# Latent attention: value products in three passes of split operands, the mask as rows, maxima and sums by transfers

## The chip, the cores and the metric

The kernel runs on one core of a Trainium2 chip. The metric is the device time of one execution in microseconds. TensorE does matrix products, VectorE (DVE), ScalarE (ACT) and GpSimd (POOL) elementwise work, and SyncE (SP) issues the transfers between the core's memory and the chip's main memory. Each engine works through its own list of instructions in order and waits on semaphores for the others.

## The reference

One layer of a streaming encoder in float32: 2048 prompt tokens and 64 sample tokens. An input projection feeds two mixers. Mixer A is latent attention (8 heads, 64 + 32 columns for scores, 64 for values), mixer B a sliding window attention. Both go through an output projection, a norm and a gated feed-forward network. The change is in mixer A:

```python
def mla_attend(qn, qp, k_nope, kpe, v, mask):
    s = (jnp.einsum('bqhd,bkhd->bhqk', qn, k_nope)
         + jnp.einsum('bqhr,bkr->bhqk', qp, kpe)).astype(jnp.float32) * MLA_SCALE
    if mask is not None:
        s = jnp.where(mask, s, NEG_INF)
    p = jax.nn.softmax(s, axis=-1).astype(v.dtype)
    return jnp.einsum('bhqk,bkhd->bqhd', p, v)
```

The mask lets a query see the keys of its own chunk of 64 tokens and of all earlier chunks. The sample tokens see 128 cached tokens and each other, without a mask.

## The kernel before

The program has three blocks, with a barrier of all engines between them: `project_inputs` (to 372 us), `attention` (to 1067 us) and `mix_and_ffn` (the rest). In `attention` the window attention comes first, then the latent attention (`latent_attention`), from 514.9 us on.

**fp32r and fp32.** A float32 product is done either as one product of kind fp32, or as three passes of kind fp32r: each operand is split into a high part, which is what fp32r keeps of it, and a low part, the rest, and high x high, high x low and low x high are added up. Projections and scores use three passes of fp32r. The value product (L1446) uses one product of kind fp32, which the trace shows as two records.

**Tiling of a head.** Queries are taken in units of 512 columns (u = 0 to 3) and one of 64 columns (u = 4, the sample), in the order 0, 4, 1, 2, 3; `pos` is the place in this order. A unit needs all key tiles of 128 up to its own last one: 42 tiles in a head, numbered s = 0 to 41. Unit 3, for instance, has tiles 26 to 41. On the diagonal a tile has 512, 384, 256 or 128 columns. So 28 tiles have 512 columns, four each have 384, 256 and 128, two have 64.

**A step.** In step s TensorE writes the scores of tile s in three passes (`score_tile`, L1426), keys on the partitions, queries along the columns; then zero to two maximum products (`max_chunk`, L1403), which are scores of a later unit with queries on the partitions and up to 512 keys along the columns, in one pass; and then the value product of tile s - 3 (LAG = 3). ScalarE takes the exponential of tile s from PSUM (L1495). There are three banks for scores, two for maximum products, two for outputs.

**Maxima.** VectorE reduces each maximum product (L1542, and L1544 for the half of a diagonal block that fewer queries see), joins the parts (L1552), TensorE turns the result into a row by four transposes (L1412) and ScalarE copies it with its sign changed into row 96 of the queries (L1486). Row 96 of the keys is one, so the score product subtracts the maximum by itself. `SPANS` says over which steps the maximum products of a unit are spread, `ROWS` at which step its row is made.

**Mask.** On a diagonal tile, GpSimd overwrites a block of 64x64 probabilities with zeros (L1387), and the value product waits for it.

**Sums.** The weights of the value product are 128 columns, the values in 64 and ones in the other 64, so its output has the head's result on 64 partitions and the sum of the probabilities on each of the other 64. ScalarE copies it out of PSUM (L1502), VectorE takes the reciprocals of 64 partitions in pieces of 128 columns (L1562), multiplies (L1571), and SyncE stores (L1347).

**Loads.** Queries, keys and values of the next head are loaded at its predecessor's step 1 with 7 transfers (`load_head`, L2274 to L2286). Heads are done in pairs: the first and last pair are written out, the two in between are a loop. At the end of the stage, ScalarE and VectorE already prepare the first tiles for `mix_and_ffn`.

## Time and profile before

| | us |
|---|---|
| median of three runs | 2862.89 |
| lowest and highest | 2862.08 to 2865.33 |
| the profiled execution | 2869.5 |
| its span | 2867.7 |
| TensorE busy in the span | 2729.4 |
| VectorE, ScalarE, GpSimd busy | 1889.1, 1306.4, 321.1 |
| latent attention, first score product to last value product's copy | 514.90 to 1060.3 |

A profile is one execution. PE is TensorE's products, PEld its weight loads, which overlap them. Records of products overlap, since each includes the way through the array: the rate is read from the distance of starts. The granted clock is TensorE's share of full speed (1.0 is 2.4 GHz). `97*128 97x512` is a product of 97 rows with 128 columns of weights and 512 moving columns. In brackets stands the idle time before an instruction and who ended it.

### The profile page before, as it was taken

What the parts mean: (1) busy time and instruction counts of PE and PEld (TensorE: products, weight loads), DVE (VectorE), ACT (ScalarE), POOL (GpSimd) and SP (SyncE); (2) the same over time, 40 slices, a digit from 0 to 9 for tenths busy, and PEclk for the clock granted to TensorE, in tenths of its full rate; (3) what the DMA queues carried; (4) which work ended last, traced back from release to release, by engine and by line L of the source; (5) the groups of instructions that cost most, each with busy time, mean ns of one, the idle gap of its engine ahead of it and who ended that gap; (6) DMA issues with size and microseconds to landing.
All of it is one profiled execution on the core that took longest, in us unless ns stands there. A gap on an engine that the chain in (4) does not pass through costs nothing.

```text
span 2867.7 us, 42705 instructions
## 1 busy us (share of the span) xinstructions
PE 2729.4 (95%) x13401; PEld 2417.4 (84%) x13401; DVE 1889.1 (66%) x2677; ACT 1306.4 (46%) x2725; POOL 321.1 (11%) x352
## 2 busy tenths in 40 slices
PE   8999978999999988999999999999999999999996
PEld 7888944666666658899999999999999999999996
DVE  6877677666666655777558754587546875468743
ACT  4443267433333434554445443454434544346531
POOL 0111021000000004000101012010120101200002
PEclk9999989899999999999999999999999999999998
DMA  7666555322223213334323533335333353324332
GB/s 220 203 204 227 188 169 154 74 55 57 55 54 62 62 63 125 103 111 143 118 96 114 183 111 116 97 111 185 113 111 104 110 182 118 112 101 136 120 122 76
DMA packets 170703, 348.65 MB, mean 122 GB/s; under 512 B 43892, under 2 KB 112852, under 8 KB 169268
## 3 DMA queue, kind: packets, MB, share of 16 engines
q1 hardware_dynamic: 170580, 347.06, 38.9%
q8 instruction: 71, 1.16, 0.2%
q14 instruction: 52, 0.43, 0.0%
HBM read 292.56 MB, written 55.30 MB: 121 GB/s over the span
## 4 chain that ended last, share of the span: by engine, by line
PE 54%; DVE 3%; issue 2%; DMA 1%; ACT 1%; POOL 1%; SPq 0%; POOLq 0%; ACTq 0%; DVEq 0%
PE mf_acc L2003 54%; DMA room<-in_w_up 1%; DVE mix_w_lo L2156 1%; ACT mix_w_hi L2049 1%; POOL mf_ss L1961 1%; PE mf_st L2041 0%; DVE mf_x L2174 0%; DMA room<-in_w_out 0%; DVE mf_xn L2207 0%; DVE mf_x L2179 0%; POOL mf_y L1986 0%; DVE mix_a_lo L2212 0%; ACT mf_sq L2072 0%; ACT mf_sq L2106 0%; DVE mf_rstd L2191 0%
## 5 line engine op out<-in xcount | busy, mean ns | idle before, releaser
L2156 DVE TENSOR_TENSOR mix_w_lo<-room,mix_w_hi 128x1024 fp32r<-128x1024 f32 (+1 forms) x338 | 470.9, 1393 | 557.8 <-ACT mix_w_hi L2049 557.1
L2003 PE MATMUL mf_acc<-mix_a_hi,mix_w_hi 128*128 128x424 f32 (+1 forms) x2016 | 724.3, 359 | 28.6 <-DVE mix_a_lo L2186 8.8
L2003 PE MATMUL mf_acc<-mix_a_hi,mix_w_lo 128*128 128x424 f32 (+1 forms) x2016 | 717.5, 356 | 0.0
L2003 PE MATMUL mf_acc<-mix_a_lo,mix_w_hi 128*128 128x424 f32 (+1 forms) x2016 | 717.1, 356 | 0.0
L2049 ACT ACTIVATE mix_w_hi<-room 128x1024 fp32r<-128x1024 f32 (+1 forms) x338 | 383.1, 1133 | 520.2 <-PE mf_acc L2003 488.9
L2003 PEld LDWEIGHTS mf_acc<-mix_a_hi,mix_w_hi 128*128 128x128 f32 x2016 | 381.8, 189 | 44.2 <-issue 11.8
L2003 PEld LDWEIGHTS mf_acc<-mix_a_hi,mix_w_lo 128*128 128x128 f32 x2016 | 382.4, 190 | 11.1
L2003 PEld LDWEIGHTS mf_acc<-mix_a_lo,mix_w_hi 128*128 128x128 f32 x2016 | 382.1, 190 | 9.3 <-issue 0.7
L1426 PE MATMUL at_ps<-ahead_q,ahead_k 97*128 97x512 f32 (+5 forms) x1008 | 362.1, 468 | 0.9 <-ACT ahead_q L1486 0.9
L2003 PE MATMUL mf_acc<-mf_h_hi,mix_w_hi 128*128 128x424 f32 (+1 forms) x944 | 339.0, 359 | 6.8 <-DVE mix_w_lo L2156 3.8
L2003 PE MATMUL mf_acc<-mf_h_hi,mix_w_lo 128*128 128x424 f32 (+1 forms) x944 | 335.2, 355 | 0.0
L2003 PE MATMUL mf_acc<-mf_h_lo,mix_w_hi 128*128 128x424 f32 (+1 forms) x944 | 334.7, 355 | 0.0
L1495 ACT ACTIVATE la_prob<-at_ps 128x512 f32<-128x512 f32 (+1 forms) x336 | 174.1, 518 | 322.0 <-PE at_ps L1426 321.4
L1446 PE MATMUL at_ps<-la_prob,ahead_v 128*128 128x512 f32 (+5 forms) x672 | 294.5, 520 | 0.0
L1426 PEld LDWEIGHTS at_ps<-ahead_q,ahead_k 97*128 97x128 f32 (+1 forms) x1008 | 180.4, 190 | 130.9 <-issue 95.7
L1542 DVE TENSOR_REDUCE la_part<-at_ps 128x1 f32<-128x512 f32 (+5 forms) x328 | 183.9, 573 | 155.7 <-PE at_ps L1403 152.9
L1961 POOL TENSOR_TENSOR mf_ss<-mf_sq,mf_ss 128x424 f32<-128x424 f32 (+1 forms) x105 | 145.5, 1386 | 478.6 <-ACT mf_sq L2072 348.7
L2003 PEld LDWEIGHTS mf_acc<-mf_h_hi,mix_w_hi 128*128 128x128 f32 x944 | 177.9, 188 | 14.8 <-DVE mix_w_lo L2156 4.9
L2003 PEld LDWEIGHTS mf_acc<-mf_h_lo,mix_w_hi 128*128 128x128 f32 x944 | 177.8, 188 | 6.1 <-issue 1.7
L2003 PEld LDWEIGHTS mf_acc<-mf_h_hi,mix_w_lo 128*128 128x128 f32 x944 | 177.7, 188 | 4.4
L768 PE MATMUL pi_acc<-pi_x_hi,pi_w_hi 128*128 128x424 f32 (+1 forms) x400 | 147.0, 367 | 22.5 <-DVE pi_x_lo L547 16.9
L2230 DVE SCALAR_TENSOR_TENSOR mf_cv<-mf_u,mf_conv_w,mf_cv 128x424 f32<-128x424 f32 (+1 forms) x220 | 145.0, 659 | 31.2 <-DVE mf_cv L2227 27.5
(186 smaller groups left out, 3542.8 us busy)
## 6 DMA issues: line engine op xcount, KB each, us to landing
room<-in_w_up SPq DMA_DIRECT2D x220, 512.0 KB, 3.5
room<-in_w_down SPq DMA_DIRECT2D x80, 704.0 KB, 4.0
pi_w_raw<-in_w_in SPq DMA_DIRECT2D x49, 512.0 KB, 6.0
room<-in_w_out SPq DMA_DIRECT2D x40, 512.0 KB, 3.5
ahead_k<-kn_scr SPq DMA_DIRECT2D x7, 1120.0 KB, 14.6
ahead_q<-qn_scr SPq DMA_DIRECT2D x7, 1056.0 KB, 7.9
room<-in_x SPq DMA_DIRECT2D x4, 1696.0 KB, 11.9
qn_scr<-pi_ring SPq DMA_DIRECT2D x16, 424.0 KB
```

The costliest lines, as they stand in the source:

```text
L768: mm = pe.matmul(acc[:, g, 0:n], w[:, s, k], x[:, par, k, 0:n], start=(k == 0 and m == 0), stop=(k == KD - 1 and m == 2))
L1426: mm = pe.matmul(out, k[0:KR, p, a, c0:c0 + keys], q[0:KR, p, b, n0 + off:n0 + n], start=(term == 0), stop=(term == 2))
L1446: pe.matmul(ov[:, (5 * p + pos) % 2, off:n], v[0:keys, p, vt], prob[0:keys, (NKT * p + s) % RING, off:n], start=(m == 0), stop=(s == last_ ...
L1495: act.activation(prob[0:keys, (NKT * p + s) % RING, off:n], sc[0:keys, s % 3, off:n], ACT.Exp, scale=MLA_SCALE).then_inc(exp_done, 1)
L1542: op = dve.tensor_reduce(part[0:rows, par, t, slot:slot + 1], sx[0:rows, bank, 0:seen], AX_X, ALU.max)
L1961: pool.tensor_tensor(ss[:, kind, 0:n], sq[:, slot, 0:n], zeros[:, 0:n] if first else ss[:, kind, 0:n], ALU.add).then_inc(sq_added, 1)
L2003: mm = pe.matmul(acc[:, t_bank[0], 0:n], w[:, g, k], x[:, k, 0:n], start=(first and k == 0 and m == 0), stop=(last and k == count - 1 and ...
L2049: act.activation(w_hi[:, g, 0:count], w_raw[:, g, 0:count], ACT.Copy).then_inc(w_hi_made, 1)
L2156: dve.tensor_tensor(w_lo[:, g, 0:count], w_raw[:, g, 0:count], w_hi[:, g, 0:count].bitcast(F32), ALU.subtract).then_inc(w_split, 1)
L2230: dve.scalar_tensor_tensor(out=out, in0=u[:, g, 1:n + 1], scalar=conv_w[:, 1, bass.ds(f, 1)], in1=out, op0=ALU.mult, op1=ALU.add).then_inc ...
```

## The change

The value product becomes three passes of fp32r with 96 columns of weights: 64 of the values' high part with 32 ones (columns 0 to 95), then 64 of the low part with 32 zeros, and the first ones again with the probabilities' low part. ScalarE takes each exponential twice, once to fp32 (`prob`, 4 buffers of which 3 are used) and once to fp32r (`high`), and one engine writes the difference (`low`): GpSimd at every third step, VectorE at the others. The values are split by ScalarE and GpSimd ahead of each head.

The mask is 16 rows more in queries and keys: row r is one in the first half of query tile r, and -2^100 in the second half of key tile r. The maximum goes to a 17th row, of which the keys hold -1. `SPANS` and `ROWS` are earlier.

The maxima are turned by VectorE in blocks of 32x32, and SyncE writes the row with four transfers (two for the sample). A unit's sum is one row, taken to the main memory (`sums_out`), back on 32 partitions (`sums_in`), inverted there, taken out again (`rec_out`) and spread over 128 partitions (`rec_in`); GpSimd multiplies, SyncE stores. These happen 1, 3, 5, 7, 9 and 10 steps after the unit's last value product. The loads of a head become 20 transfers of 8 rows, one a step, and 10 for values. In the feed-forward and in the window attention some semaphores are merged, and the last stores of the window attention move into the first steps of the latent one.

The diff, cut to this core (`prob[...]`, `high`, `low` are rings of tiles; "..." marks what is left out):

```diff
+HIDE = -2.0 ** 100
...
+V_LO = slice(V_DIM + 32, 2 * V_DIM + 32)
...
+            pool.memset(ahead["v"][:, g, :, V_DIM:V_LO.start].bitcast(F32), 1.0).then_inc(rows_set, 1)
+            pool.memset(ahead["v"][:, g, :, V_LO.stop:].bitcast(F32), 0.0).then_inc(rows_set, 1)
...
+        diagonal = ident[HD:MR, HD:MR].rearrange("r (t o) -> r t o", o=1).broadcast_to([MR - HD, SEQ // P, CHUNK])
+        for g in range(2):
+            halves = [x[HD:MR, g, 0, 0:SEQ].rearrange("r (t e c) -> r t e c", e=2, c=CHUNK)
+                      for x in (ahead["q"], ahead["k"])]
+            pool.tensor_scalar(halves[0][:, :, 0], diagonal, 1.0, None, ALU.mult).then_inc(rows_set, 1)
+            pool.tensor_scalar(halves[1][:, :, 1], diagonal, HIDE, None, ALU.mult).then_inc(rows_set, 1)
+        pool.wait_ge(rows_set, 17)
...
-    SPANS = {3: (0, 10), 4: (12, 22), 0: (24, 27), 1: (28, 28), 2: (29, 37)}
-    ROWS = {3: 12, 4: 24, 0: 31, 1: 32, 2: 39}
+    SPANS = {3: (0, 9), 4: (10, 21), 0: (22, 26), 1: (27, 27), 2: (28, 36)}
+    ROWS = {3: 10, 4: 22, 0: 27, 1: 28, 2: 37}
...
+    FIRST_OF_POOL = 9
+
+    def on_pool(i, p, s):
+
...
+    def split_low(eng, i, p, s, done):
+
+        pos, m = tiles[s]
+        _, keys, _, off = key_tiles(ORDER[pos])[m]
+        if on_pool(i, p, s):
+            keys = P
+        n, x = cols(ORDER[pos])[1], NKT * p + s
+        eng.wait_ge(exp_done, tile_no(i, p, s) + 1)
+        ge(eng, pv_done, tile_no(i, p, s) + 1 - RING)
+        eng.tensor_tensor(low[0:keys, x % RING, off:n], prob[0:keys, x % RAWS, off:n],
+                          high[0:keys, x % RING, off:n].bitcast(F32), ALU.subtract).then_inc(done, 1)
...
+        def sums_out(i, p, pos):
+            a, _, n, y = chain(i, p, pos)
+            sp.wait_ge(kept, y + 1)
+            sp.dma_start(d["sum_scr"][a:a + 1, 0:n], raw[V_DIM:V_DIM + 1, a, 0:n]).then_inc(moved[a], 16)
+
+        def sums_in(i, p, pos):
+            a, base, n, _ = chain(i, p, pos)
+            sp.wait_ge(moved[a], base + 16)
+            sp.dma_start(sums[0:n // CE, a],
+                         d["sum_scr"][a][0:n].rearrange("(c e) -> c e", e=CE)).then_inc(moved[a], 16)
+
+        def rec_out(i, p, pos):
+            a, _, n, y = chain(i, p, pos)
+            sp.wait_ge(rec_done, y + 1)
+            sp.dma_start(d["inv_scr"][a][0:n].rearrange("(c e) -> c e", e=CE), rec[0:n // CE, a]).then_inc(moved[a], 16)
+
+        def rec_in(i, p, pos):
+            a, base, n, _ = chain(i, p, pos)
+            sp.wait_ge(moved[a], base + 48)
+            row = bass.AP(tensor=d["inv_scr"].tensor, offset=a * UQ, ap=[[0, P], [1, n]])
+            sp.dma_start(rec_all[:, a, 0:n], row).then_inc(moved[a], 16)
+
         def store(i, p, pos):
...
+            sp.wait_ge(turned, 2 * y + 2)
+            ge(sp, row_in[a], 16 * (rows_of_parity(i, p, pos) - row_parts(pos)))
+            for e in range(row_parts(pos)):
+                if u < 4:
+                    to = q[MR:MR + 1, p, 0, n0:n0 + UQ].bitcast(F32).rearrange("o (t c) -> o t c", t=QT)[:, :, Q4 * e:Q4 * e + Q4]
+                    sp.dma_start(to, turned_top[Q4 * e:Q4 * e + QT, a]).then_inc(row_in[a], 16)
...
-            if s == 1 and more:
-                j, g = following(i, p)
-                ge(sp, pv_done, tile_no(i, p, 0))
-                load_head(sp, d, ahead, j, g, head_in[g], range(HEAD_DMAS))
+            for unit in rows_at(i, p, s, more):
+                row(*unit)
+            for unit in after(i, p, s, 1):
+                sums_out(*unit)
+            for unit in after(i, p, s, 3):
+                sums_in(*unit)
+            for unit in after(i, p, s, 5):
+                rec_out(*unit)
+            for unit in after(i, p, s, 7):
+                rec_in(*unit)
+            for unit in after(i, p, s, 10):
+                store(*unit)
+            if more:
+                load(i, p, s)
...
-        def max_row(i, p, pos):
-
-            y = unit_no(i, p, pos)
-            pe.wait_ge(top_done, y + 1)
-            ge(pe, row_set, y)
-            for t in range(QT if ORDER[pos] < 4 else 1):
-                mm = pe.transpose(mt[0:1, t * P:(t + 1) * P], top[:, (5 * p + pos) % 2, t:t + 1], ident[:])
-            mm.then_inc(mt_done, 1)
+            pe.matmul(sx[0:rows, (NCH * p + first_chunk[pos] + m) % 2, 0:n], q[0:MR, p, 0, q0:q0 + rows],
...
-            for term, (a, b) in enumerate(((0, 0), (0, 1), (1, 0))):
-                mm = pe.matmul(out, k[0:KR, p, a, c0:c0 + keys], q[0:KR, p, b, n0 + off:n0 + n],
+            for term, (a, b, rows) in enumerate(((0, 0, MR + 1), (0, 1, HD), (1, 0, HD))):
+                mm = pe.matmul(out, k[0:rows, p, a, c0:c0 + keys], q[0:rows, p, b, n0 + off:n0 + n],
                                start=(term == 0), stop=(term == 2))
...
-            if diag:
-                pe.wait_ge(masked, 2 * len(diagonal) * i + len(diagonal) * p + diagonal.index(s) + 1)
-            else:
-                pe.wait_ge(exp_done, tile_no(i, p, s) + 1)
-            pe.matmul(ov[:, (5 * p + pos) % 2, off:n], v[0:keys, p, vt], prob[0:keys, (NKT * p + s) % RING, off:n],
-                      start=(m == 0), stop=(s == last_tile[pos]), skip_group_check=True).then_inc(pv_done, 1)
+                ge(pe, kept, unit_no(i, p, pos) - 1)
+            if s == 0:
+                if at_first(i, p):
+                    pe.wait_ge(wa["ov_kept"], wa["tiles"])
+                    pe.wait_ge(wa["rec_kept"], wa["tiles"])
+                pe.wait_ge(v_split, 3 * (2 * i + p) + 3)
+            out, hi, lo = ov[0:V_LO.start, parity(p, pos), off:n], high[0:keys, slot, off:n], low[0:keys, slot, off:n]
+            pe.wait_ge(exp_done, tile_no(i, p, s) + 1)
+            pe.matmul(out, v[0:keys, p, vt, 0:V_LO.start], hi, start=(m == 0), stop=False, skip_group_check=True)
+            pe.matmul(out, v[0:keys, p, vt, V_LO.start:], hi, start=False, stop=False, skip_group_check=True)
+            wait_low(pe, i, p, s)
+            pe.matmul(out, v[0:keys, p, vt, 0:V_LO.start], lo, start=False, stop=(s == last_tile[pos]),
+                      skip_group_check=True).then_inc(pv_done, 1)
...
+            earlier = back(i, p, s, RAWS)
+            if earlier:
+                wait_low(act, *earlier)
+            ge(act, pv_done, tile_no(i, p, s) + 1 - RING)
+            act.activation(prob[0:keys, x % RAWS, off:n], sc[0:keys, s % 3, off:n], ACT.Exp, scale=MLA_SCALE)
+            act.activation(high[0:keys, x % RING, off:n], sc[0:keys, s % 3, off:n], ACT.Exp,
                            scale=MLA_SCALE).then_inc(exp_done, 1)
 
...
+            dve.wait_ge(turned, 2 * y + 1)
+            ge(dve, row_in[a], 16 * (rows_of_parity(i, p, pos) - row_parts(pos)))
+            dve.transpose(turned_top[:, a], top[:, a]).then_inc(turned, 1)
+
+        def invert(i, p, pos):
+            n, a = cols(ORDER[pos])[1], place(p, pos)
+            dve.wait_ge(moved[a], 80 * earlier_there(i, p, pos) + 32)
+            dve.reciprocal(rec[0:n // CE, a], sums[0:n // CE, a]).then_inc(rec_done, 1)
...
-            for i_, p_, pos, t, n in norms(i, p, s):
-                invert(i_, p_, pos, t, n)
-                if t == n - 1:
-                    norm(i_, p_, pos)
+            if at_first(i, p) and s == 6:
+                dve.memset(raw[V_LO.start:P, 0:3], 0.0)
+            if not on_pool(i, p, s):
+                split_low(dve, i, p, s, low_dve)
+            for unit in after(i, p, s, 5):
+                invert(*unit)
...
+            pool.wait_ge(moved[a], 80 * earlier_there(i, p, pos) + 64)
+            pool.tensor_tensor(raw[:, a, 0:n], raw[:, a, 0:n], rec_all[:, a, 0:n],
+                               ALU.mult).then_inc(normed, 1)
+
         def step(i, p, s, more):
-            if s in diagonal:
-                x = tile_no(i, p, s)
-                _, _, _, off, _ = key_tiles(ORDER[tiles[s][0]])[tiles[s][1]]
-                pool.wait_ge(exp_done, x + 1)
```

TensorE, first head, two steps around the start of the unit u = 1 (tile 6), before. L1426 are scores, L1403 maximum products, L1412 transposes, L1446 values:

```order
L1403 MATMUL at_ps<-ahead_k,ahead_q 128x512 [waits la_sx_free]
L1412 MATMUL at_ps<-early_ident,la_top 1x128 [waits la_row_set,la_top_done]
L1412 MATMUL at_ps<-early_ident,la_top 1x128 x3
L1446 MATMUL at_ps<-la_prob,ahead_v 128x256 [waits la_masked]
L1426 MATMUL at_ps<-ahead_q,ahead_k 128x512 [waits la_exp_done,la_row_set]
L1426 MATMUL at_ps<-ahead_q,ahead_k 128x512 x2
L1403 MATMUL at_ps<-ahead_k,ahead_q 128x128 [waits la_sx_free]
L1403 MATMUL at_ps<-ahead_k,ahead_q 128x512 [waits la_sx_free]
L1446 MATMUL at_ps<-la_prob,ahead_v 128x128 [waits la_masked]
```

The same place now, L1636 scores, L1622 maximum products, L1655, L1656 and L1658 the three passes for the values:

```order
L1636 MATMUL at_ps<-ahead_q,ahead_k 128x512 [waits la_exp_done,la_row_in0]
L1636 MATMUL at_ps<-ahead_q,ahead_k 128x512 x2
L1622 MATMUL at_ps<-ahead_k,ahead_q 128x512 [waits la_sx_free]
L1655 MATMUL at_ps<-la_high,ahead_v 96x128 [waits la_exp_done]
L1656 MATMUL at_ps<-la_high,ahead_v 96x128
L1658 MATMUL at_ps<-la_low,ahead_v 96x128 [waits la_low_dve]
L1636 MATMUL at_ps<-ahead_q,ahead_k 128x512 [waits la_exp_done]
L1636 MATMUL at_ps<-ahead_q,ahead_k 128x512 x2
L1622 MATMUL at_ps<-ahead_k,ahead_q 128x512 [waits la_sx_free]
L1622 MATMUL at_ps<-ahead_k,ahead_q 128x256 [waits la_sx_free]
L1655 MATMUL at_ps<-la_high,ahead_v 96x64 [waits la_exp_done]
```

The transposes are gone, the first score product of a unit waits for transfers (`la_row_in0`), and each value product has become three, the last of which waits for the low part of VectorE or GpSimd.

VectorE, first head, in the middle, before. L1542 and L1544 are maxima, L1552 joins them, L1562 and L1571 are reciprocals and scaling:

```order
L1562 RECIPROCAL la_rec<-wa_prob 64x128
L1542 TENSOR_REDUCE la_part<-at_ps 128x1 [waits la_sx_done]
L1562 RECIPROCAL la_rec<-wa_prob 64x128
L1542 TENSOR_REDUCE la_part<-at_ps 128x1 [waits la_sx_done] x2
L1544 TENSOR_REDUCE la_part<-at_ps 64x1
L1552 TENSOR_REDUCE la_top<-la_part 128x4 [waits la_sx_free]
L1562 RECIPROCAL la_rec<-wa_prob 64x128
L1571 TENSOR_TENSOR la_att<-wa_prob,la_rec 64x512 [waits la_rec_done]
L1542 TENSOR_REDUCE la_part<-at_ps 128x1 [waits la_sx_done]
L1562 RECIPROCAL la_rec<-wa_prob 64x64 [waits la_ov_kept,la_normed]
L1571 TENSOR_TENSOR la_att<-wa_prob,la_rec 64x64 [waits la_rec_done]
```

The same engine now in the second head, steps 5 to 10. L1737 are maxima, L1442 low parts, L1745 and L1749 join and turn maxima, L1754 is the short reciprocal:

```order
L1737 TENSOR_REDUCE la_part<-at_ps 128x1 [waits la_sx_done]
L1442 TENSOR_TENSOR la_low<-la_prob,la_high 128x512 [waits la_pv_done,la_exp_done]
L1737 TENSOR_REDUCE la_part<-at_ps 128x1 [waits la_sx_done] x2
L1442 TENSOR_TENSOR la_low<-la_prob,la_high 128x512 [waits la_pv_done,la_exp_done]
L1754 RECIPROCAL la_rec<-la_sums 32x16 [waits la_moved0]
L1737 TENSOR_REDUCE la_part<-at_ps 128x1 [waits la_sx_done]
L1442 TENSOR_TENSOR la_low<-la_prob,la_high 128x512 [waits la_pv_done,la_exp_done]
L1737 TENSOR_REDUCE la_part<-at_ps 128x1 [waits la_sx_done] x2
L1745 TENSOR_REDUCE la_top<-la_part 128x4 [waits la_sx_free]
L1749 STREAM_TRANSPOSE la_turned_top<-la_top 128x32 [waits la_row_in1,la_turned]
L1442 TENSOR_TENSOR la_low<-la_prob,la_high 128x512 [waits la_pv_done,la_exp_done] x2
```

Between the maxima now stand subtractions that wait for ScalarE's exponential of the same step, where reciprocals stood that wait for a kept output at most.

SyncE, first head now, steps 19 to 25; before, it issued nothing there but a store. L1463, L1469, L1475 and L1481 are `sums_in`, `rec_out`, `rec_in` and `store`, L1493 a row of maxima, L1519 values:

```order
L1463 DMA la_sums<-sum_scr 32x16 [waits la_moved2]
L1513 DMA ahead_k<-kn_scr 8x4480 [waits la_sc_done] x2
L1469 DMA inv_scr<-la_rec 32x16 [waits la_rec_done]
L1519 DMA ahead_v<-vt_scr 128x2x64
L1493 DMA ahead_q<-la_turned_top 1x4x32 [waits la_row_in0,la_turned]
L1493 DMA ahead_q<-la_turned_top 1x4x32 x3
L1519 DMA ahead_v<-vt_scr 128x2x64 [waits la_sc_done]
L1475 DMA la_rec_all<-inv_scr 128x512 [waits la_moved2]
L1519 DMA ahead_v<-vt_scr 128x2x64 [waits la_sc_done] x3
L1481 DMA att_scr<-la_raw 64x512 [waits la_normed]
L1519 DMA ahead_v<-vt_scr 128x2x64 [waits la_sc_done]
L1493 DMA ahead_q<-la_turned_top 1x4x32 [waits la_row_in1,la_turned]
```

The row for tile 26 (L1493, `la_row_in0`) stands behind `rec_out`, which waits for VectorE, and a load of values.

## Rows read from the trace of the kernel before

**Rows 1.** Windows of the latent attention; per engine busy us (instructions), then granted clock.

```profile
560.00:700.00 140.00, 135.94 (x557) 91.08 (x555) 92.93 (x175) 54.59 (x108) 10.28 (x34) 1.00 0.28 57
...
980.00:1068.00 88.00, 78.15 (x304) 51.19 (x303) 53.98 (x87) 35.66 (x70) 7.02 (x23) 0.97 0.13 41
```

**Rows 2.** Groups by form, 514 to 1062 us: count, busy us and mean ns, idle before.

```profile
L1426 PE MATMUL at_ps<-ahead_q,ahead_k 97*128 97x512 f32 x672 | 262.9, 499 | 0.9 <-ACT ahead_q L1486 0.9
L1446 PE MATMUL at_ps<-la_prob,ahead_v 128*128 128x512 f32 x448 | 230.3, 595 | 0.0
...
L1495 ACT ACTIVATE la_prob<-at_ps 128x512 f32<-128x512 f32 x224 | 133.7, 597 | 227.1 <-PE at_ps L1426 226.5
L1542 DVE TENSOR_REDUCE la_part<-at_ps 128x1 f32<-128x512 f32 x192 | 130.1, 686 | 112.5 <-PE at_ps L1403 110.9
L1562 DVE RECIPROCAL la_rec<-wa_prob 64x128 f32<-64x128 f32 x126 | 117.8, 940 | 15.8 <-ACT wa_prob L1502 13.5
```

**Rows 3.** Timeline of TensorE in head 3: start us, length us, instruction, count.

```profile
702.70 1.02 PE L1446 MATMUL at_ps<-la_prob,ahead_v 128*128 128x512 f32 x2
703.15 1.26 PE L1426 MATMUL at_ps<-ahead_q,ahead_k 97*128 97x512 f32 x3
704.26 0.39 PE L1403 MATMUL at_ps<-ahead_k,ahead_q 96*128 96x512 f32 x1
704.49 1.02 PE L1446 MATMUL at_ps<-la_prob,ahead_v 128*128 128x512 f32 x2
...
706.09 0.60 PE L1412 MATMUL at_ps<-early_ident,la_top 128*1 128x128 f32 x4
706.53 1.02 PE L1446 MATMUL at_ps<-la_prob,ahead_v 128*128 128x512 f32 x2
```

**Rows 4.** Timeline, ScalarE: first output of two successive heads kept.

```profile
664.88 0.59 ACT L1502 ACTIVATE wa_prob<-at_ps 128x512 f32<-128x512 f32 x1
...
733.29 0.59 ACT L1502 ACTIVATE wa_prob<-at_ps 128x512 f32<-128x512 f32 x1
```

**Rows 5.** Timeline, weight loads in one head, with idle before them and releaser.

```profile
670.08 0.19 PEld L1403 LDWEIGHTS at_ps<-ahead_k,ahead_q 96*128 96x128 f32 x1 [1.57 <-DVE la_part L1542]
...
677.19 0.19 PEld L1403 LDWEIGHTS at_ps<-ahead_k,ahead_q 96*128 96x128 f32 x1 [0.56 <-DVE la_part L1542]
...
680.27 0.19 PEld L1403 LDWEIGHTS at_ps<-ahead_k,ahead_q 96*128 96x128 f32 x1 [1.79 <-DVE la_part L1542]
```

**Rows 6.** Timeline in the next block: GpSimd and VectorE, together and apart.

```profile
1126.13 1.27 POOL L1961 TENSOR_TENSOR mf_ss<-mf_sq,mf_ss 128x424 f32<-128x424 f32 x1
...
1126.48 1.38 DVE L2179 TENSOR_TENSOR mf_x<-mf_x 128x424 f32<-128x424 f32 x1
...
1133.37 0.60 DVE L2179 TENSOR_TENSOR mf_x<-mf_x 128x424 f32<-128x424 f32 x1
```

**Rows 7.** Timeline, ScalarE, window attention: two operations back to back.

```profile
508.74 1.08 ACT L1118 ACTIVATE wa_probT<-at_ps 128x512 f32<-128x512 f32 x2 [1.23 <-PE at_ps L1051]
```

**Rows 8.** Timeline, GpSimd, its first product in the window attention.

```profile
390.03 1.27 POOL L1016 TENSOR_TENSOR wa_outT<-wa_outT,wa_rec_all 128x512 f32<-128x512 f32 x1 [4.22 <-DMA wa_rec_all<-rec_scr]
```

**Rows 9.** Transfers issued, whole span: count, KB each, median us to landing.

```profile
wa_rec_all<-rec_scr SPq DMA_DIRECT2D x32, 128.0 KB, 2.9
...
att_scr<-la_att SPq DMA_DIRECT2D x8, 16.0 KB, 1.7
```

**Rows 10.** Timeline: first score product; then the end of the stage.

```profile
514.90 1.65 PE L1426 MATMUL at_ps<-ahead_q,ahead_k 97*128 97x512 f32 x3 [0.68 <-ACT ahead_q L1486]
...
1059.65 0.60 ACT L1502 ACTIVATE wa_prob<-at_ps 128x512 f32<-128x512 f32 x1 [1.99 <-PE at_ps L1446]
1060.34 3.38 DVE L1562 RECIPROCAL la_rec<-wa_prob 64x128 f32<-64x128 f32 x4 [13.04 <-ACT wa_prob L1502]
...
1064.55 0.47 SPq L1347 DMA_DIRECT2D att_scr<-la_att  x1
...
1067.45 0.69 PE L2003 MATMUL mf_acc<-mix_a_hi,mix_w_hi 128*128 128x424 f32 x1 [7.90 <-ACTq L2052]
```

521 lines of the change are left out of this document (286 added, 235 removed).

## The prediction

> **What bounds the kernel now.** I read the windows first. In the latent attention, from 514.9 us to 1060 us of the span, TensorE is busy 135.94 of 140 us at full granted clock [rows 1], so what counts there is TensorE's own work and what it waits for. Then the groups of this stretch: score products of 512 columns, fp32 value products of 512 columns, one exponential per tile of 597 ns, maxima of 686 ns, and 126 reciprocals of 940 ns [rows 2]. Then one step of TensorE in order of time [rows 3]: value product at 702.70, three score passes, one maximum product at 704.26, the next value product at 704.49. One 512-column pass of the fp32r kind takes 704.49 - 704.26 = 0.23 us. The step is 1.79 us, so the fp32 value product (two records) takes 1.79 - 4 x 0.23 = 0.87 us. Records overlap, so I go by starts, not by durations. The four transposes of a row of maxima take 706.53 - 706.09 = 0.44 us. Last, the period of one head: the first output of a head is kept at 664.88 and of the next at 733.29, 68.4 us [rows 4]; 545 us over eight heads is 68.1. TensorE's waits for VectorE in such a head are 1.57 + 0.56 + 1.79 = 3.9 us [rows 5], all in its first quarter, where VectorE has reciprocals between the maxima.
>
> **Value products.** A head has 42 tiles of keys: 28 with 512 columns, four each with 384, 256 and 128, two with 64. Each gets three fp32r passes for the fp32 product. At 512 columns that is 0.69 for 0.87 us, -0.18 us, 28 times: -5.0. In proportion, 384 columns save 0.13 and 256 save 0.09, four times each: -0.9. For 128 and 64 columns I assume that a pass doesn't fall below 0.1 us, which costs 4 x 0.1 + 2 x 0.15 = +0.7. Sum -5.2 us a head. Bounds: the passes could be as dear as in proportion to the records (then -4), or the narrow ones free of that floor (-5.9).
>
> **Row of maxima.** Four units of four transposes and one of one leave TensorE: 4 x 0.44 + 0.1 = -1.9 us a head. The row now goes VectorE, SyncE, queue, memory. TensorE therefore does 7.1 us less in a head, 57 us in eight.
>
> **Mask.** The 128 small fills on GpSimd and the second, 64-row maximum on each diagonal block go. The mask is 17 more rows of the score and maximum products, which have the same number of columns: nothing on TensorE. The filled rows are made on GpSimd at the start of the window attention; that is perhaps 10 us more than now there, before its first product at 390.03 [rows 8], whose result is stored some 6 us later. I put it at nothing, with 3 us as its upper end.
>
> **ScalarE.** It does each exponential twice. Two 512-column operations back to back take 1.08 us [rows 7], so ScalarE has about 28 x 1.08 + 10 for the narrow tiles + 3 for outputs + 2 for the values' high parts = 45 us a head. In a step of 1.61 us (seven passes of 0.23) that fits beside the products.
>
> **VectorE.** It loses the reciprocals (15.7 us a head by [rows 2]), the scaling and the small maxima, and gets the low parts of two tiles in three. A subtraction of 424 columns takes 0.60 us [rows 6]; scaled to 512, 0.70 us. 19 wide tiles x 0.70 + 9 narrow ones = 16.5 us. Maxima 24, joining and transposing them 1.9, short reciprocals 1: 43.4 us a head, about what it has now. But the order is stiff: the subtraction of tile s waits for both exponentials of s, and the maxima of the next step stand behind it; TensorE's second maximum product from there waits for these. A subtraction ends about 2.7 us after its step began, which leaves the maxima on time with one block a step. Where a step has two blocks or is short (steps 0 to 9: 11.4 us of VectorE against 12.2 us of TensorE by the same durations) it does not.
>
> **GpSimd.** One low part in three and all scaling: 128x512 takes 1.27 us [rows 8], 14 + 5 + 3 operations, some 26 us of 60. Tile s is needed 3 steps later, 4.8 us, of which the exponentials and 1.3 us use 3.4. It hides, with 1.4 us to spare.
>
> What is shared shows in [rows 6]: while GpSimd runs an operation at 1126.13, VectorE's subtraction at 1126.48 takes 1.38 us, and the same one takes 0.60 at 1133.37. So a GpSimd operation can lengthen a VectorE operation by up to 0.8 us. I count a third of the 22 with 0.8, about 6 us of VectorE time in a head, most of it in its free time. The Trainium skill, "SBUF — State Buffer", section "Who interferes with whom", says that a VectorE instruction with two SBUF inputs contends with a GpSimd instruction that reads SBUF, and that the one that starts first holds the shared ports for its whole length. The trace agrees with 1.38 against 0.60 us. By this rule all 22 could strike, since both engines now do exactly such subtractions, and the sum would go over to the second rival below.
>
> **Transfers.** A head has 20 loads of queries and keys where there were 3, 10 of values for 4, 18 parts of rows, and 25 steps of the sums' chain for 5 stores. At about 0.3 to 0.6 us an issue I estimate 30 us of SyncE in 60, but in order, and with waits for landings. A landing takes 1.7 us for 16 KB to 2.9 us for the spread of 128 KB over partitions [rows 9]; the new spread has 256 KB. For the last unit of a head the row is issued at step 22 and read at step 26, 6.6 us later by 0.23 us passes; SyncE stands at step 21 until VectorE's short reciprocal (4.5 us after step 21 began), then a load of values, then four parts: about 8.7 us against 8.2. So 0.5 us and up to 1 is waited there, and at the unit that starts at tile 14 the same count leaves 1 us of slack.
>
> TensorE's waits in a head are then, in my estimate, 3 us behind the maxima, 1 us for a row, 1.5 us of small ones: 5.5 for 3.9, +1.6 x 8 = +13 us. Bounds: 2 us a head (no reciprocals, all hidden: -15 us) and 11 us (VectorE full all along: +57 us).
>
> **The start and the end.** The first score product at 514.90 waits for a row from ScalarE [rows 10]; the row now needs four transfers, which can be issued before the last window tile is through. With the first values made on GpSimd and short distances in the first head I take +1 us, between -1 and +5. The end is plain: now the last output is kept at 1059.65, four reciprocals to 1063.7, the store issued at 1064.55, TensorE resumes at 1067.45 [rows 10], 7.8 us. Instead: keep 0.6, sum out 1.9, sum in 1.9, reciprocal 0.3, out 1.9, spread 2.9, scaling 1.3, store and block end 2.9 = 13.7 us: +6. Nothing hides it; every engine waits at the end of the block.
>
> **Sum.** -57 + 13 + 1 + 6 = -37 us. Against this execution's 2869.5 us (span 2867.7) that is 2832.5; the runs' median is 6.6 us lower, so I predict 2826 us. With waits from 3.5 to 8 us a head in place of 5.5 this case reaches from 2810 to 2846.
>
> **Rivals.**
> One: the waits vanish, since what delays maxima today are the reciprocals (the last four take 3.38 us together [rows 10]), and those are gone. For it: VectorE is at 72%. Against: the stiff order. Then 2 us a head in place of 5.5: 2826 - 28 = 2798, up to 2810.
>
> Two, the other side: VectorE becomes the bound of the whole stage, by GpSimd's operations holding it up. 43.4 us + 22 x 0.8 = 61 us a head, plus what it idles waiting for exponentials, 6 to 8 us, gives 67 to 69 us a head, where the forecast has 68.1 - 7.1 + 1.6 = 62.6. At 69 us the stage loses 7 us and the start and end cost 7 more: +14, 2877 us. It decides the sign from 67.2 us a head. For it: [rows 6]. Against: only a third of the tiles go to GpSimd, and they are distributed evenly, where VectorE has just maxima, which read PSUM.
>
> Three: rows come late at every unit, since SyncE must wait for landings of the sums' chain ahead of them. 2 us at two of five units a head is +32 us less the 8 that I have: 2850; 1 us more at each gives 2860.
>
> Four: the passes are not full rate with 96 columns of weights or 113 rows, and the value products cost 0.87 us as before. Then -57 shrinks to -15 and the time is 2868. The score products with 97 rows at 0.23 us speak against it.
>
> **How the numbers follow.** Forecast 0.55, one 0.16, two 0.14, three 0.12, four 0.03. Range 2801 to 2864: it takes in most of one and three, leaves two out. A measurement of this kernel tells about 0.2% (6 us) from no change: case two and four give slower 0.15, the edge of three and four gives same 0.05, the rest is faster, 0.80.
>
> **What would show it.** Right: a 512-column step of 1.6 us with one maximum; a period of 60 to 63 us a head; 13 to 14 us between the last kept output and TensorE's next product; clock 1.0 through the stage. Wrong: maxima products that wait over 6 us a head for VectorE, subtractions on VectorE with a mean over 0.9 us at 512 columns (two), score products that wait for the queue at tiles 14 and 26 (three), value passes more than 0.25 us apart (four). A head over 67 us overturns the sign. The sum rests most on the 0.18 us a tile and on the waits.

## The result, and the profile after

| | median us | runs | ratio to before, 95% interval |
|---|---|---|---|
| before | 2864.1 | 2862.1 to 2872.5 | |
| changed kernel | 2911.9 | 2910.2 to 2916.0 | 1.0163, 1.0140 to 1.0187 |

The changed kernel is 48 us slower; 2826 us was forecast. The profiled execution has a span of 2914.2 us, 46.5 more than before, and this is where they lie. The first score product starts at 512.22 us instead of 514.90 [rows 10], 2.7 us earlier. This isn't won by the change: TensorE's first product of the window attention is at 367.82 us instead of 372.27, behind a block that the change leaves as it was, and from there to the first score product 144.4 us pass instead of 142.6, so 1.8 are lost. From the first score product to the copy of the last value product 592.5 us pass instead of 544.8: 47.7 lost, where the sum had 44 won. The end takes 12.4 us instead of 7.8: 4.6 lost, where 6 were forecast. The rest of the program is 3 us shorter.

The window that answers to [rows 1] (same columns), and the groups that answer to [rows 2]:

```profile
560.00:700.00 140.00, 122.54 (x569) 96.10 (x568) 87.97 (x164) 80.26 (x179) 48.67 (x43) 0.93 0.37 69
```

```profile
L1737 DVE TENSOR_REDUCE la_part<-at_ps 128x1 f32<-128x512 f32 x223 | 150.3, 683 | 70.5 <-PE at_ps L1622 68.4
...
L1442 DVE TENSOR_TENSOR la_low<-la_prob,la_high 128x512 fp32r<-128x512 f32 x153 | 118.0, 773 | 38.0 <-ACT la_high L1695 30.4 <-PE at_ps L1658 6.2
L1636 PE MATMUL at_ps<-ahead_q,ahead_k 113*128 113x512 f32 x223 | 97.0, 435 | 19.1 <-DMA ahead_q<-la_turned_top 19.0
...
L1442 POOL TENSOR_TENSOR la_low<-la_prob,la_high 128x512 fp32r<-128x512 f32 x71 | 93.0, 1310 | 185.2 <-ACT la_high L1695 154.2 <-PE at_ps L1658 31.0
```

TensorE stands still for 17.5 of 140 us where it stood for 4, and its granted clock is 0.93 for 1.00. VectorE is less busy than before (87.97 for 92.93 us), so it isn't the bound by its work. The timeline of TensorE that answers to [rows 3] shows that the passes are what the prediction took them for, 0.23 us from start to start:

```profile
703.16 0.40 PE L1622 MATMUL at_ps<-ahead_k,ahead_q 112*128 112x512 f32 x1
703.39 0.39 PE L1655 MATMUL at_ps<-la_high,ahead_v 128*96 128x512 f32 x1
703.62 0.39 PE L1656 MATMUL at_ps<-la_high,ahead_v 128*96 128x512 f32 x1
703.85 0.39 PE L1658 MATMUL at_ps<-la_low,ahead_v 128*96 128x512 f32 x1
704.08 0.87 PE L1636 MATMUL at_ps<-ahead_q,ahead_k 113*128 113x512 f32 x3
```

What TensorE waited for from 514 us to 1080 us (us in total, times, longest), first the products, then the weight loads, which partly count the same waits again:

```profile
PE at_ps L1622 <- DVE la_part L1737: 21.1, 18, 2.5
PE at_ps L1622 <- DMA ahead_k<-kn_scr: 19.6, 4, 6.2
PE at_ps L1636 <- DMA ahead_q<-la_turned_top: 18.0, 8, 3.3
PE at_ps L1622 <- issue: 13.1, 3, 4.8
```

```profile
PEld at_ps L1622 <- issue: 34.8, 7, 6.5
PEld at_ps L1622 <- DVE la_part L1737: 29.5, 27, 2.9
PEld at_ps L1636 <- DMA ahead_q<-la_turned_top: 12.1, 4, 3.7
```

The third line is scores that wait for a row of maxima. Seven waits of a maximum product, one a head, are the first product of the next head, which waits for that head's keys: for four of them the profile names the keys' transfer, for three it names nobody ("issue"), but they stand at the same product of 128 columns. In all the products wait 21.1 + 19.6 + 18.0 + 13.1 = 71.8 us, 9.0 us a head. Here is one wait for keys, with SyncE's issues ahead of it and the granted clock behind it:

```profile
704.98 0.82 SPq L1513 DMA_DIRECT2D ahead_k<-kn_scr  x2
```

```profile
707.36 0.70 PE L1636 MATMUL at_ps<-ahead_q,ahead_k 113*128 113x384 f32 x3
711.31 0.32 PE L1622 MATMUL at_ps<-ahead_k,ahead_q 112*128 112x128 f32 x1 [3.26 <-DMA ahead_k<-kn_scr]
```

```profile
709.00:711.00 2.00, 0.00 (x0) 0.00 (x0) 0.96 (x2) 0.09 (x1) 0.99 (x1) 1.00 0.03 10
711.00:713.00 2.00, 1.69 (x8) 1.45 (x9) 0.29 (x1) 0.00 (x0) 0.00 (x0) 0.77 0.16 37
713.00:715.00 2.00, 2.00 (x9) 1.60 (x8) 0.85 (x2) 0.66 (x2) 0.00 (x0) 0.50 0.01 1
715.00:717.00 2.00, 2.00 (x9) 1.64 (x9) 0.76 (x2) 0.45 (x2) 0.00 (x0) 0.87 0.42 106
```

The keys' last pieces are issued by 705.8, the product starts at 711.31. After the standstill the clock falls from 1.00 (2.4 GHz) to 0.50 (1.2 GHz); in windows of 0.5 us it is 1.00 again from 715.5 on, 4.2 us after the product. Summed over the windows above, that is another (0.23 + 0.50 + 0.13) x 2 = 1.7 us for a wait of 3.3. Two first outputs of successive heads are kept at 671.04 and 744.83, a period of 73.8 us for 68.4 [rows 4]; the mean over eight heads is 74.1.

### The profile page after: what moved, and what is told of

Same layout as the page of the kernel before. It is cut to its first block, busy times and chain, and to the rows that moved or that the text cites. A ratio compares the mean times of both kernels' runs of the same rounds, so it can differ in the third digit from the quotient of the medians.

```text
span 2914.2 us, 45192 instructions
## 1 busy us (share of the span) xinstructions
PE 2711.3 (93%) x13601; PEld 2462.7 (85%) x13601; DVE 1889.7 (65%) x2681; ACT 1428.1 (49%) x3042; POOL 494.6 (17%) x409
## 4 chain that ended last, share of the span: by engine, by line
PE 53%; DVE 3%; issue 2%; ACT 1%; DMA 1%; POOL 1%; SPq 0%; POOLq 0%; ACTq 0%; DVEq 0%
PE mf_acc L2186 53%; DVE mix_w_lo L2339 1%; DMA room<-in_w_up 1%; ACT mix_w_hi L2232 1%; POOL mf_ss L2144 1%; PE mf_st L2224 0%; DMA room<-in_w_out 0%; DVE mf_x L2357 0%; DVE mf_xn L2390 0%; DVE mf_x L2362 0%; POOL mf_y L2169 0%; DVE mix_a_lo L2395 0%; ACT mf_sq L2255 0%; ACT mf_sq L2289 0%; DVE mf_rstd L2374 0%
## 5 line engine op out<-in xcount | busy, mean ns | idle before, releaser
L2186 PE MATMUL mf_acc<-mix_a_hi,mix_w_hi 128*128 128x424 f32 (+1 forms) x2016 | 723.9, 359 | 30.5 <-ACTq L2235 12.4
L1636 PE MATMUL at_ps<-ahead_q,ahead_k 96*128 96x512 f32 (+8 forms) x1008 | 273.9, 383 | 20.8 <-DMA ahead_q<-la_turned_top 20.8
L1737 DVE TENSOR_REDUCE la_part<-at_ps 128x1 f32<-128x512 f32 (+4 forms) x328 | 190.2, 596 | 118.0 <-PE at_ps L1622 115.1
L1636 PEld LDWEIGHTS at_ps<-ahead_q,ahead_k 96*128 96x128 f32 (+2 forms) x1008 | 190.2, 203 | 65.3 <-DMA ahead_q<-la_turned_top 15.5
L1442 DVE TENSOR_TENSOR la_low<-la_prob,la_high 128x512 fp32r<-128x512 f32 (+3 forms) x227 | 164.5, 728 | 50.3 <-ACT la_high L1695 41.3
L1622 PE MATMUL at_ps<-ahead_k,ahead_q 112*128 112x512 f32 (+4 forms) x328 | 124.8, 405 | 55.8 <-DVE la_part L1737 23.1
L1695 ACT ACTIVATE la_high<-at_ps 128x512 fp32r<-128x512 f32 (+1 forms) x336 | 174.1, 518 | 0.0
```

What stands on the lines that cost most here:

```text
L1442: eng.tensor_tensor(low[0:keys, x % RING, off:n], prob[0:keys, x % RAWS, off:n], high[0:keys, x % RING, off:n].bitcast(F32), ALU.subtract) ...
L1622: pe.matmul(sx[0:rows, (NCH * p + first_chunk[pos] + m) % 2, 0:n], q[0:MR, p, 0, q0:q0 + rows], k[0:MR, p, 0, c0:c0 + n], start=True, stop ...
L1636: mm = pe.matmul(out, k[0:rows, p, a, c0:c0 + keys], q[0:rows, p, b, n0 + off:n0 + n], start=(term == 0), stop=(term == 2))
L1695: act.activation(high[0:keys, x % RING, off:n], sc[0:keys, s % 3, off:n], ACT.Exp, scale=MLA_SCALE).then_inc(exp_done, 1)
L1737: dve.tensor_reduce(part[0:rows, parity(p, pos), t, slot:slot + 1], sx[0:rows, bank, 0:n], AX_X, ALU.max).then_inc(sx_free, 1)
L2186: mm = pe.matmul(acc[:, t_bank[0], 0:n], w[:, g, k], x[:, k, 0:n], start=(first and k == 0 and m == 0), stop=(last and k == count - 1 and ...
```

## The experiments

Times are medians of the runs, ratios go by the kernel before.

| run | us | ratio, 95% interval |
|---|---|---|
| e1 two loads a step | 2983.5 | 1.0428, 1.0382 to 1.0474 |
| e2 spaced chain | 2939.4 | 1.0239, 1.0203 to 1.0275 |
| e3 both | 2967.1 | 1.0345, 1.0310 to 1.0380 |
| e4 fp32 values | 2927.5 | 1.0219, 1.0197 to 1.0241 |
| e5 loads on ScalarE's queue | 2950.8 | 1.0297, 1.0273 to 1.0321 |
| e6 late chain | 2907.6 | 1.0145, 1.0121 to 1.0170 |
| e7 late chain, loads on ScalarE | 2923.6 | 1.0205, 1.0184 to 1.0225 |
| e8 rows on TensorE | 2903.5 | 1.0145, 1.0123 to 1.0168 |
| e9 pieces of 16 rows | 2865.3 | 0.9995, 0.9985 to 1.0005 |
| e10 whole loads | 2904.4 | 1.0129, 1.0110 to 1.0147 |
| e11 16 rows, late chain | 2828.2 | 0.9865, 0.9848 to 0.9881 |
| e12 16 rows, rows on TensorE | 2829.3 | 0.9874, 0.9857 to 0.9890 |
| e13 half pieces of 16 rows | 2858.2 | 0.9981, 0.9969 to 0.9993 |
| e14 e9 with fp32 values | 2849.7 | 0.9946, 0.9930 to 0.9963 |
| e15 16 rows, late chain, rows on TensorE | 2821.5 | 0.9850, 0.9834 to 0.9866 |
| e16 e15 with half pieces | 2829.0 | 0.9871, 0.9854 to 0.9887 |
| e17 e15 with fp32 values | 2857.0 | 0.9969, 0.9956 to 0.9981 |
| e18 e15 with pieces of 8 rows | 2901.0 | 1.0127, 1.0111 to 1.0144 |

**The order in the list.** The first theory (A) was that SyncE's one list is late: it stood some 250 us of the stage waiting inside the sums' chain, and each row part takes 0.60 to 0.65 us to issue.

e1 issued the pieces earlier:

```
-            if 1 <= s <= QK_DMAS:
+            for x in range(2 * s - 1, 2 * s + 1) if 1 <= s <= QK_DMAS // 2 else ():
```

> The twenty query and key loads of the next head are issued two a step in steps 1 to 10, in place of one a step in steps 1 to 20; all else as in the changed kernel. Theory A (SyncE's one list in order is late: the key loads keep the first maximum product of 7 heads waiting 3.3 to 6.2 us each, and TensorE then runs at half clock for about 5 us): those seven waits go, about 33 us of waiting and some 15 us of clock, so 2865 to 2880 us against 2912; the waits of the first maximum product for the key transfer vanish from the trace. Theory B (what costs is VectorE: subtractions of 0.77 us beside maxima): under 8 us gained, 2904 to 2912. Theory C (the same list only has its lateness moved: the sums' chain and the rows are pushed back by the burst of loads): key waits vanish but the row waits of the score products grow, 2890 to 2910.

e2 moved the chain's steps apart:

```
-            for unit in after(i, p, s, 1):
+            for unit in after(i, p, s, 2):
                 sums_out(*unit)
-            for unit in after(i, p, s, 5):
+            for unit in after(i, p, s, 7):
                 rec_out(*unit)
...
```

> The steps of the sums' chain are placed later, so that each finds its input there: sums out at 2 (was 1), sums in 4 (3), inversion 6 (5), inverted sums out 7 (5), spread 9 (7), multiplication 11 (9), store 13 (10). The same instructions, no fewer. Theory A: SyncE stood 250 us of the stage waiting inside this chain; without that the loads and rows are issued on their step, the key waits and most row waits go, 2850 to 2875 us. Theory B (VectorE): VectorE no longer stands 53 us waiting for the sums, which it would gain too: 2880 to 2900 with the waits of the maxima products shrunk and those for keys left. If neither the spacing nor the order matters: 2905 to 2915.

e3 had both:

> The two edits before together. Theory A: no wait for keys, row waits under 1 us each, clock 1.0 through most of the stage: 2835 to 2862 us, at or under the kernel before (2864). Theory B: the floor set by VectorE stays, 2880 to 2900. If the row transfers themselves (four issues of 0.65 us and a landing) are too long for the place they have, the row waits remain: 2860 to 2885.

All three were slower than the changed kernel, by 72, 27 and 55 us, so A as it stood fell. e1's trace says why. These are waits of 514 us to 1110 us, TensorE's and then VectorE's; lines have moved by one:

```profile
PE at_ps L1623 <- DVE la_part L1738: 79.4, 14, 8.9
```

```profile
DVE la_rec L1755 <- DMA la_sums<-sum_scr: 108.8, 24, 8.9
```

The key waits are gone, but the sums land later: VectorE stands 109 us at the reciprocal (53 in the changed kernel), the maxima stand behind it, and TensorE waits for them. The rows come later too (36.2 us of waits for 19.0). With more loads in flight the small transfers were later. In e2 SyncE waited 56.8 us for the sums to land (31.1 in the changed kernel) and ScalarE 41 us for places. Theory D made of this: what counts is that VectorE stands at the reciprocal.

**Which part of the change.** e4 leaves the passes out:

```
-            act.activation(prob[0:keys, x % RAWS, off:n], sc[0:keys, s % 3, off:n], ACT.Exp, scale=MLA_SCALE)
...
-            pe.matmul(out, v[0:keys, p, vt, 0:V_LO.start], hi, start=(m == 0), stop=False, skip_group_check=True)
-            pe.matmul(out, v[0:keys, p, vt, V_LO.start:], hi, start=False, stop=False, skip_group_check=True)
-            wait_low(pe, i, p, s)
...
+            pe.matmul(out, v[0:keys, p, vt, V_LO.start:].bitcast(F32), high[0:keys, slot, off:n].bitcast(F32),
```

> The changed kernel without the three passes: one exponential a tile, the value product as one fp32 product of probabilities and values (as in the kernel before), no low parts on VectorE or GpSimd, no splitting of the values; the mask rows, the maxima and the sums by transfers and all loads as in the changed kernel. Theory A (transfers cost): it stays slow, the key and row waits are there: the 57 us of cheaper products and transposes shrink by the products' 42 us, so 2900 to 2950. Theory B (the low parts on VectorE cost): 2840 to 2870, no more than the kernel before.

2927 us: what is left without the passes, the transfers above all, makes the kernel slow without any low part. The rival that blamed the low parts on VectorE was out.

**The lists relieved.** e5 moved the loads to ScalarE's queue (`load(act, i, p, s)` after `exp_tile`), e6 gave the chain a fourth place and more time for each input, e7 did both. The edit of e6, in which the chain's steps become 1, 4, 8 (inversion), 9, 12, 15 (scaling) and 17 (store) instead of 1, 3, 5, 5, 7, 9 and 10:

```
-    PLACES = (0, 1, 2, 0, 1, 2, 0, 1, 0, 2)
+    PLACES = (0, 1, 2, 3, 0, 1, 2, 3, 0, 3)
...
-            for unit in after(i, p, s, 5):
+            for unit in after(i, p, s, 8):
                 invert(*unit)
```

> The thirty query, key and value loads of a head are issued from ScalarE's queue, after the exponentials of the same step, in place of SyncE's; the sums' chain, the stores and the rows stay on SyncE. ScalarE gets 30 issues of 0.3 to 0.5 us, some 11 us a head beside 48 us of work in 84. Theory A (one list in order: every load waits behind the chain's waits): key waits of the first maximum product go, 7 of 4.8 us with the half clock after each, and SyncE has 11 us a head more: 2865 to 2885 us. Theory D, new after the two first runs (what costs is that VectorE stands at the reciprocal for the sums' transfer, 53 us in the changed kernel and 109 with two loads a step, and the maxima queue behind it): the key waits go but VectorE's wait stays 40 to 60 us, 2880 to 2900. If transfers themselves are slow (the queue's bandwidth): no change, 2905 to 2920.

> Four places for kept outputs in place of three, and the sums' chain at steps 1, 4, 8 (inversion), 9, 12, 15 (multiplication), 17 (store) after a unit, in place of 1, 3, 5, 5, 7, 9, 10; loads and rows stay on SyncE. Theory D: VectorE no longer waits for the sums (under 10 us in all), nor does SyncE for VectorE and GpSimd; the maxima come in time: 2850 to 2880 us. Theory A also expects it, if the chain's waits are what made the list late. Rival: the row's four issues of 0.65 us and the loads by themselves keep the list late: waits for keys and rows stay over 30 us, 2890 to 2910.

> Both edits. Theories A and D together: no wait for keys, none for the sums on VectorE, row waits under 1 us; clock 1.0: 2825 to 2855 us, faster than the kernel before (2864). If it stays over 2880 something else than lists in order holds TensorE up.

e5 was 39 us slower than the changed kernel: the loads, no longer held back by SyncE's waits, came earlier and the sums later, and VectorE stood 78.8 us at the reciprocal (53 in the changed kernel, 109 in e1). In e6 VectorE hardly waited for the sums any more (5.7 us in all), and yet the kernel gained only 4 us, while its key waits rose from 32.7 to 39.8 us: D fell as the cause of the loss too. e7 showed what was left. The last key piece in ScalarE's list, and TensorE's next maximum product:

```profile
710.23 0.30 ACTq L1460 DMA_DIRECT2D ahead_k<-kn_scr  x1
```

```profile
719.14 0.47 PE L1616 MATMUL at_ps<-ahead_k,ahead_q 112*128 112x128 f32 x1 [4.56 <-DMA ahead_k<-kn_scr]
```

Nothing held the issue of the piece up in its list, and yet its 140 KB were used only 8.9 us later. This was no matter of order in a list. But it isn't the time of one piece alone: pieces had been issued before it, about one a step. The head's first piece was issued at 676.82, so the issues of the twenty took 33.4 us, but from the first issue to the use of the last 42.3 us pass, 2.1 us a piece with all that ran beside them. The last piece stood in a queue of pieces.

e8 gave the row of maxima back to TensorE: `max_row` on TensorE and `row` on ScalarE as in the kernel before, its steps too, no transpose on VectorE, no row parts on SyncE; the mask's rows moved up by one.

> The maxima's row is made as in the kernel before (four transposes on TensorE, a copy on ScalarE, at the steps of the kernel before), the mask stays rows of the score product (one row later), the three passes and the sums by transfers stay. SyncE has 18 issues of 0.65 us a head less, 12 us. Theory A (the row issues and the chain's waits make the list late): row waits go, key waits shrink below 1 us, 2850 to 2875 us though the transposes cost 15 us in all. Theory D (VectorE at the reciprocal): stays, 2885 to 2905.

It won 8 us and kept key waits (15.2 us in 6). That they are shorter can be its steps: `SPANS` of the kernel before asks for the next head's keys at step 24 in place of 22.

**The shape of the pieces.** The kernel before loads a head in whole transfers, 64 rows of queries, 32, and 64 of keys, and the keys land 14.6 us after issue. The changed kernel loads the same 2.7 MB in pieces of 8 rows. e9 makes them 16 rows, e10 loads whole:

```
-            if 1 <= s <= QK_DMAS:
...
-                if s <= 8:
-                    r = 8 * (s - 1)
-                    sp.dma_start(q[r:r + 8, g, :, 0:TOK]..., d["qn_scr"][...][r:r + 8])
...
+            for x in [x for x, at in enumerate((1, 3, 5, ..., 19)) if at == s]:
...
+                if x < 4:
+                    r = 16 * x
+                    sp.dma_start(q[r:r + 16, g, :, 0:TOK]..., d["qn_scr"][...][r:r + 16])
...
```

> The next head's queries and keys are loaded in ten pieces of 16 rows (280 KB) at steps 1, 3, ... 19 in place of twenty pieces of 8 rows (140 KB) at steps 1 to 20: the same bytes over the same steps, half the issues, all else as in the changed kernel. Theory Q, new after e7 (there the last key piece is issued at 710.23 us and the product that waits for it starts at 719.14, 8.9 us later, with nothing ahead of it in ScalarE's list): pieces of 8 rows do not keep all 16 DMA engines busy (share 0.5 and 70 to 120 GB/s in the loading stretches of the changed kernel, against 1.0 and 231 GB/s for the whole loads of the kernel before), one a step is as much as they carry, and keys, sums and rows land behind one another. Then wide pieces take the key waits away and shorten the waits for sums and rows: 2840 to 2875 us. Theory A (SyncE's list) expects only ten issues of 0.3 us a head: 2900 to 2912. If it is no change, Q falls.

> Queries and keys of the next head in three whole transfers at step 1 (as in the kernel before, where they land 14.6 us after issue); the rest as in the changed kernel. Theory Q: no key waits; the sums and rows of steps 1 to 12 land behind 2.8 MB, a few us late once a head (the chain of the last unit, the row for tile 14): 2850 to 2885 us. Theory A: seventeen issues less, but no more than 10 us: 2900 to 2910.

> The pieces of 16 rows with the late chain and four places of e6 (2907.6). Theory Q: without backlog in the queue the late chain has slack at each step, VectorE and SyncE wait little: 2830 to 2860 us. If the rows remain late through SyncE's waits: 2860 to 2880.

> The pieces of 16 rows with the maxima's row by TensorE of e8 (2903.5): what is left of the change is the passes and the sums by transfers. Theory Q: 2835 to 2865 us; the row by transfer or by TensorE then makes a difference of at most 15 us either way against e9.

e9 gave back 47 us, all of the loss. e10 missed its range by 19 us: the key waits went, but the small transfers landed behind a load of 14.4 us, and SyncE waited 71.3 us in 8 waits, up to 12.2, for the sums. So in this kernel the loads must be wide and spread over the steps. On top of e9 the late chain (e11) is worth 37 us and the rows on TensorE (e12) 36, where by themselves they were worth 4 and 8. Both come out under their ranges, by 2 and 6 us.

e13 is the sharpest of the runs: twenty pieces of the same bytes at the same steps, and only the shape is changed.

```
-                if s <= 8:
-                    r = 8 * (s - 1)
-                    sp.dma_start(q[r:r + 8, g, :, 0:TOK]..., d["qn_scr"][...][r:r + 8])
...
+                x, e = (s - 1) // 2, (s - 1) % 2
+                if x < 4:
+                    r = 16 * x
+                    sp.dma_start(q[r:r + 16, g, e, 0:TOK]..., d["qn_scr"][...][r:r + 16, e])
...
```

> Twenty pieces at steps 1 to 20 as in the changed kernel and of the same 140 KB, but each of 16 rows and one half (high or low) in place of 8 rows and both halves. Theory Q (8 rows do not fill the DMA engines, so the queue backs up): as e9, 2850 to 2880 us, no key waits. If it was the number of issues on SyncE: as the changed kernel, 2900 to 2915.

2858 us: 54 under the changed kernel. The forecast of no key waits was too good: 15.5 us of them are left in 6 waits (32.7 in 7 in the changed kernel), where e9, whose last piece goes out a step earlier, has none. A piece of 140 KB lands after 3.7 us (of e13's 48 key pieces; the last row is min/median/max):

```profile
L1514 SPq DMA_DIRECT2D ahead_k<-kn_scr x48: 323/361/1326, 612.8 to 946.2; - x48
...
DMA to landing us min/median/max: 3.2/3.7/5.7
```

So it is the shape and not the number of issues. How much a shape carries shows in windows in which loads follow one another. The last three columns are granted clock, mean busy share of the 16 DMA engines, and GB/s. Pieces of 8 rows in the changed kernel, the same in e18 (below), and the kernel before while its whole loads run (64 and 32 rows, and the values):

```profile
672.00:684.00 12.00, 10.88 (x58) 8.50 (x57) 9.01 (x19) 6.84 (x17) 1.64 (x3) 1.00 0.45 71
```

```profile
666.00:676.00 10.00, 10.00 (x52) 7.76 (x52) 7.82 (x15) 7.97 (x19) 2.30 (x2) 1.00 0.52 68
```

```profile
660.00:672.00 12.00, 10.87 (x49) 7.68 (x48) 10.69 (x18) 4.20 (x10) 0.32 (x2) 1.00 1.01 221
```

At 68 GB/s a piece of 132 or 140 KB takes 2.0 to 2.1 us (an estimate from the second line), as in e7, and the change puts one into each step of 1.6 us. That gives a queue that grows by some 0.4 us a piece, 8 us over the twenty, and keys, sums and rows land behind it.

The Trainium skill, "DMA: Bandwidth & Descriptors", section "Why a DMA increments its semaphore by 16 and not by 1", gives a reason: a transfer runs on as many of the 16 DMA engines as the largest number up to 16 that divides the slowest dimension of both its sides, and on this queue always on the lowest-numbered ones; 8 rows then use 8 engines, 16 rows all. The runs agree with it: a busy share of 0.52 against 1.01. No view here shows single DMA engines, so that those eight are the ones that also carry rows and sums is what the Trainium skill says and no run shows. Half the engines alone would leave some 110 of 221 GB/s and not 68; what takes the rest, no run shows.

**What is left of the sum.**

> e4 (one exponential, the value product as one fp32 product, no low parts) with the pieces of 16 rows. By e4's windows TensorE was idle 12 us in 140, some 50 us of the stage: Theory Q takes most of it, 2875 to 2895 us against 2927. The prediction's step on the products (5.2 us a head for the passes) then says 42 us over a version of passes that waits as little (e11 and e12 at 2828: so 2870); if the passes cost as much elsewhere as they give, it is below 2840.

> Pieces of 16 rows, the late chain and the rows on TensorE together. e11 and e12 both have TensorE busy 137 of 140 us, at clock 1.00: if both took the same waits away, 2820 to 2828 us; if different ones, under 2815.

> As e15 with the half pieces of e13. A piece of 140 KB leaves the queue in half the time of one of 280 KB, so what lands behind it is less late: at or up to 5 us under e15. If the twenty issues matter: up to 5 us over it.

> e15 (2821.5 us) with one exponential and the value product as one fp32 product, no low parts. The prediction's term, 5.2 us a head for the passes, gives 2863; if the passes' extra weight loads, exponentials and low parts cost as much as they give once nothing waits, 2820 to 2835. e14 (2849.7), where TensorE was already busy 139 of 140 us, makes 2850 to 2865 the likelier.

> e15 (2821.5 us) with the twenty pieces of 8 rows of the changed kernel. Theory Q: the keys still land some 9 us after the last issue, 7 waits of 3 to 7 us with the clock's fall after each: 2860 to 2885 us. If slack elsewhere absorbs the slow pieces: under 2835.

e15 is the best version, 44 us under the kernel before and 90 under the changed one. Its window, and the only wait of its products for another engine that sums to over 1 us in the stage (without the stage's end):

```profile
560.00:700.00 140.00, 140.00 (x714) 111.39 (x713) 97.79 (x181) 103.76 (x224) 58.46 (x51) 1.00 0.45 78
```

```profile
PE at_ps L1623 <- DVE la_part L1757: 4.0, 5, 1.7
```

Two first outputs of successive heads:

```profile
647.76 0.59 ACT L1719 ACTIVATE la_raw<-at_ps 96x512 f32<-96x512 f32 x1
...
708.21 0.59 ACT L1719 ACTIVATE la_raw<-at_ps 96x512 f32<-96x512 f32 x1
```

A period of 60.5 us; the mean from the first score product at 513.14 to the last kept output at 1011.00 is 62.2 us a head. Both are inside the 60 to 63 of the forecast. e18 puts the narrow pieces back into this version, and that costs 80 us, more than my 40 to 64: no slack elsewhere takes them up. Its key waits, where e15 has none:

```profile
PE at_ps L1621 <- DMA ahead_k<-kn_scr: 19.8, 4, 6.4
PE at_ps L1621 <- issue: 18.0, 3, 8.3
```

e17 prices the passes: 35.5 us where hardly anything waits. e14 came out under its range of 2875 to 2895 us and is 16 us under e9, though. So in e9 the gain of the passes is lost, 35.5 + 16 = 51 us. Of these, e9's products wait 41 us in the stage where e14's wait 8.5 (for rows alone 29.7 and 7.5), and its clock is 0.96 where e14's is 0.99, by an estimate another 16 us. That the slower fp32 products lengthen each step and so give the rows time is a reading that no run tests. e16 was expected at or under e15 and is not: its four runs (2822.9 to 2830.1 us) lie above those of e15 (2819.9 to 2822.7), but the intervals against the kernel before overlap, so that the half pieces cost something here stays unclear.

## Why the prediction was wrong

**The step that failed is "Transfers".** It counts the 20 loads of queries and keys "where there were 3" and prices their issues, but puts the time that they hold the queue at nothing. The landings that it has are of single transfers of 16 KB and 128 KB [rows 9]. That a piece of 8 rows carries less than its share was nowhere in it: such pieces move at 68 GB/s where whole loads move at 221, so that one takes 2.0 to 2.1 us of a step of 1.6. By e13 the shape alone is 54 us, by e18 80. The 5.5 us a head of waits were worked out from the order of the list, with none for keys; in the changed kernel they are 9.0, of which 4.1 are for keys, and the half clock comes behind each.

**The clock.** "Clock 1.0 through the stage" was wrong (0.93 in the window, 0.91 from 514 to 1060 us) because of the waits; in e15 it is 1.00 in the window and 0.98 in the stage. The sum had no price for the time behind a wait. A head takes 73.8 us where 62.6 were forecast. Of these 11.2 us the waits are 3.5 and the clock, by an estimate of 0.07 x 73.8, about 5; I can't assign the other 2 to 3.

**SyncE's issues.** A row part takes 0.60 to 0.65 us, at and over the upper end of the 0.3 to 0.6 that I took. Four of them in e7:

```profile
713.73 2.56 SPq L1514 DMA_DIRECT2D ahead_q<-la_turned_top  x4
```

The order of the list only mattered once the pieces were wide: late chain or rows on TensorE are then 36 to 37 us.

**Value products.** 5.2 us a head forecast, 4.4 measured by e17 against e15. Right in kind, the forecast 18% too high. The floor of 0.1 us for narrow passes isn't there: at full clock three passes of 128 columns start 0.06 to 0.09 us apart (696.88, 696.94 and 697.02, the next product at 697.11).

**Row of maxima off TensorE.** 15 us forecast, none measured: e15 makes it on TensorE and is 7 us under e11, which moves it by transfers (the intervals against the kernel before still overlap). That what the transposes cost is lost again in issues and late rows (4.1 us of waits for them in e11) is a reading; no run takes the two apart.

**Start and end.** +1 and +6 us forecast, +1.8 and +4.6 found, the start counted from the first product of the window attention. Right. The 2.7 us by which the stage starts earlier come from the block ahead of it, which the change doesn't touch.

**The rivals.** Two (GpSimd slows VectorE) was wrong for this kernel: the subtractions take 0.77 us in the mean, under the 0.9 that it needed, and 0.80 in e15, which hardly waits. Three (rows late behind the sums' chain) was nearest: its waits were there (18.0 us in 8, where it had 32), but its 2850 to 2860 us left out the keys. Four was wrong by the timeline. One, that waits nearly vanish, is what e15 does once the loads are mended: its products wait 4.0 us in all for maxima, its weight loads 10.2. Less the 15 us of the transposes, which it does on TensorE, it would stand at an estimated 2806, inside that rival's 2798 to 2810; that was not run, and e11 shows that the 15 us are not free to take. e11 has all of the change, with wide pieces and a late chain alone mended, and runs at 2828 us, 2 over the forecast. That it comes so close is in part luck: its products wait some 2.6 us a head where the forecast has 5.5, and the passes give less than it has.

That the range ended at 2864 was the second mistake: it took the worst of the list's order as the worst of the transfers.

## What to carry to other kernels

When a change cuts a load into pieces, look at the piece's shape before its size: here 16 rows in place of 8 on the outermost dimension were worth 54 to 80 us at the same bytes. Read the rate in GB/s in a stretch where the pieces follow one another, and compare the time of a piece with the time of a step. Before reordering a late list, find one transfer whose issue nothing held up; if that one lands late too, order in the list is not the cause. Price a wait of TensorE with the half clock that follows it (here 1.7 us for 3.3).

## What was not expected of the hardware

- Pieces of 140 KB in 8 rows, one after another: 68 GB/s at a DMA share of 0.52, and 8.9 us from the last issue to its use (e7); in 16 rows: 3.7 us to landing (e13). Whole loads: 221 GB/s at 1.01.
- With more pieces in flight the sums landed later, whichever queue issued the pieces: VectorE stood 109 us for them in e1 and 79 in e5, where the pieces are on ScalarE's queue, against 53 us.
- An issue of a row part of 4 x 128 bytes takes SyncE 0.60 to 0.65 us; of a key piece of 140 KB, 0.29.
- After 3.3 us of standstill TensorE's granted clock fell to 0.50 within 1.2 us of the next product, and it was 1.00 again 4.2 us after that product.
